# Small per-head products of a decoder step on TensorE: heads of one tile shape put side by side, sample weights on 128 partitions, squares folded twice

## What is computed

```python
s = einsum('bihd,bjhd->bijh', q, k) * exp(d)        # scores x decay: "weights"
y = einsum('bijh,bjhv->bihv', s, v) + einsum('bihd,bhdv->bihv', q, c) * exp(inter)
c_new = c * exp(b_end) + einsum('bjhd,bjhv->bhdv', k * exp(w_end), v)
...
var = square(x - mu).mean(-1)                       # LayerNorm over 1024 channels
```

## Time and profile before

| what | value |
|---|---|
| median of three runs | 1001.87 us |
| profiled execution, its own time | 997.59 us |
| its span | 995.8 us |
| granted TensorE clock, mean | 0.997 of full speed |
| TensorE matmul busy | 979.1 us (98%) |
| DVE, ACT, POOL busy | 503.0, 193.0, 81.6 us |
| layer 0: mixing block and first LayerNorm | about 32 to 206 us |
| layer 1: mixing block and first LayerNorm | about 439 to 634 us |
| experts | about 634 to 978 us |

### The profile page before, as it was taken

How to read it: one execution, slowest core, us unless ns; L and a number is a source line. 1 busy time by engine, 2 the same in 40 slices (tenths; PEclk the granted TensorE clock), 3 DMA queues, 4 the chain that set the end, 5 groups by cost and what they waited for, 6 DMA issues and landing times.

```text
span 995.8 us, 24204 instructions
## 1 busy us (share of the span) xinstructions
PE 979.1 (98%) x10904; PEld 800.4 (80%) x10904; DVE 503.0 (51%) x1032; ACT 193.0 (19%) x414; POOL 81.6 (8%) x105
## 2 busy tenths in 40 slices
PE   9999999999999999999999999999999999999995
PEld 6897887999999999997978779557776767777643
DVE  6888894755666654269878975420101201010135
ACT  1434232221111100044343332300000000000001
POOL 1110022500000000000000200230000020000020
PEclk9999999999999999999999999999999999999998
DMA  9437248224453155201243488899999999999972
GB/s 356 152 111 248 92 169 359 85 86 170 170 189 125 58 204 220 101 31 56 87 123 114 159 317 330 327 332 396 401 420 400 423 385 412 425 423 421 421 305 98
DMA packets 37500, 241.46 MB, mean 242 GB/s; under 512 B 5008, under 2 KB 8144, under 8 KB 17680
## 3 DMA queue, kind: packets, MB, share of 16 engines
q1 hardware_dynamic: 27280, 216.69, 55.4%
q0 software_dynamic: 6432, 19.43, 5.5%
q10 hardware_dynamic: 3680, 3.74, 1.2%
HBM read 228.60 MB, written 13.07 MB: 243 GB/s over the span
## 4 chain that ended last, share of the span: by engine, by line
PE 89%; DVE 8%; ACT 1%; issue 1%; DVEq 0%
PE ps L773 67%; PE ps L1384 15%; PE ps L1492 6%; PE ps L776 1%; PE ps L1321 1%; ACT up_slots L1841 0%; DVE overlay L2566 0%; DVE overlay L2512 0%; DVE small L2465 0%; ACT overlay L1841 0%; DVE overlay L2428 0%; DVE mix_or_moe L2426 0%; ACT x L1841 0%; DVE overlay L2427 0%; DVE up_slots L2546 0%
## 5 line engine op out<-in xcount | busy, mean ns | idle before, releaser
L773 PE MATMUL ps<-up_slots,mix_or_moe 128*32 128x352 f32 (+2 forms) x3248 | 241.0, 451 | 0.5 <-issue 0.4
L773 PEld LDWEIGHTS ps<-up_slots,mix_or_moe 128*32 128x32 f32 (+2 forms) x3248 | 148.5, 111 | 83.5 <-issue 10.6
L773 PE MATMUL ps<-x,up_slots 128*128 128x144 f32 (+3 forms) x832 | 152.3, 336 | 0.0
L773 PEld LDWEIGHTS ps<-x,up_slots 128*128 128x128 f32 x832 | 124.7, 190 | 25.2 <-issue 8.0
L773 PE MATMUL ps<-overlay,tables 128*32 128x256 f32 (+4 forms) x1992 | 122.6, 375 | 0.0
L773 PEld LDWEIGHTS ps<-overlay,tables 128*32 128x32 f32 (+2 forms) x1992 | 97.4, 113 | 21.2 <-issue 2.3
L3141 DVE TENSOR_TENSOR mix_or_moe<-mix_or_moe,ps 128x352 f32<-128x352 f32 x24 | 11.2, 517 | 174.7 <-PE ps L773 174.7
L1384 PE MATMUL ps<-overlay,up_slots 128*128 128x144 f32 x704 | 91.7, 286 | 0.6 <-DVE overlay L2917 0.3
L1384 PEld LDWEIGHTS ps<-overlay,up_slots 128*128 128x128 f32 x704 | 88.4, 190 | 1.1 <-issue 0.8
L773 PE MATMUL ps<-up_slots 128*128 128x144 f32 (+2 forms) x960 | 80.9, 257 | 1.2 <-DVE up_slots L2546 1.0
L773 PE MATMUL ps<-overlay,up_slots 128*128 128x128 f32 (+3 forms) x528 | 78.2, 308 | 0.0
(11 more groups left out here) (379 smaller groups left out, 1004.7 us busy)
## 6 DMA issues: line engine op xcount, KB each, us to landing
up_slots<-in_moe_w SPq DMA_DIRECT2D x64, 1408.0 KB, 22.3
overlay<-in_moe_w SPq DMA_DIRECT2D x21, 1536.0 KB, 24.1
up_slots<-in_ffn_w SPq DMA_DIRECT2D x30, 1024.0 KB, 6.9
up_slots<-in_w_in SPq DMA_DIRECT2D x27, 1024.0 KB, 5.3
up_slots<-in_w_out SPq DMA_DIRECT2D x8, 1024.0 KB, 7.0
overlay<-in_moe_w SPq DMA_DIRECT2D x7, 1024.0 KB, 23.8
mix_or_moe<-in_states POOLq DMA_DIRECT2D x6, 512.0 KB, 5.6
expert_tokens<-in_shape_tables POOLq DMA_DIRECT2D x8, 384.0 KB, 7.6
```

The costliest lines, as they stand in the source:

```text
L773: return pe.matmul(o, lhsT, rhs, start=start, stop=stop)
```

## The change

In `mix(l)` and its helpers:

- The samples' scores, decays, weights and HGRN2 intra-chunk weights of head n go to partitions 32n to 32n+31 (before: partitions 0 to 31, heads side by side in the free dimension). One product per head and one DVE or ACT operation for all four heads then stand for one per pair of heads. The tables get masks for this layout; the whole table keeps its size. The samples' values are read from `SAMPLE_VALUES` (made by `sample_rows`), and their transposes and ACT's copy of them are gone.
- Functions are split into a prompt and a sample part (`sample_scores`, `value_rows`, `key_rows`, `sample_outputs`, `sample_denominators`) and issued so that products of one tile shape follow each other.
- Panel pieces between them are joined: seven(3, 3..7) once instead of in three groups, seven(6, 0..7) in two groups instead of five, tile 16 in two instead of three. Level 5 moves ahead of the pieces of panel 3, `head_scale(C_)` of mLSTM behind HGRN2's outputs, HGRN2's sample states behind the prompt's retention states.
- `fold_squares` folds a second time (four tiles to two), and `variance` sums two tiles.

```diff
@@ variance
-                for k in range(4):
-                    last = mm(PS[:, 7, c], tb("lnmean"), SQS[q][:, k, c], k == 0, k == 3)
+                for k in range(2):
+                    last = mm(PS[:, 7, c], tb("lnmean"), SQS[q][:, k, c], k == 0, k == 1)
@@ fold_squares
-                tt(sq[:, 0:4, c], sq[:, 0:4, c], sq[:, 4:8, c], AD).then_inc(S["ln_fold"], 1)
+                link(tt(sq[:, 0:4, c], sq[:, 0:4, c], sq[:, 4:8, c], AD))
+                tt(sq[:, 0:2, c], sq[:, 0:2, c], sq[:, 2:4, c], AD).then_inc(S["ln_fold"], 1)
@@ gate_cols (TensorE)
-                    mm(PS[0:NS, C_ + 1, 0:NH], rli[:, SEQ:T], ident[:, 0:P:HR])
-                    for n in range(NH):
-                        last = mm(PS[NS * n:NS * n + NS, C_ + 1, NH:NH + 1], rtmp[:, SEQ:T], ident[:, HR * n:HR * n + 1])
+                    for k, row in enumerate((rli, rtmp)):
+                        for n in range(NH):
+                            last = mm(PS[NS * n:NS * n + NS, C_ + 1, k:k + 1], row[:, SEQ:T], ident[:, HR * n:HR * n + 1])
@@ decays
-                        mm(o[:, SEQ + P:WS], ident, tb("causal_sample"), False, False)
+                    if h0 == 0:
+                        mm(PS[:, bank, SEQ + P:WS], ident, tb("causal_sample"), False, False)
+                        mm(PS[:, bank, SEQ + P:WS], tb("headrows"), rb[:, SEQ:T], False, False)
...
-                    for o, sel, row in heads:
-                        last = mm(o[:, SEQ + P:WS], sel, row[:, SEQ:T], False, True)
@@ new
+                def sample_scores(bank, q, k):
+                    for n in range(NH):
+                        at, i = rows_of(n)
+                        r = slice(at, at + HD)
+                        last = mm(PS[NS * n:NS * n + NS, bank, SEQ + P:WS], proj[r, k + i, SEQ:T], proj[r, q + i, SEQ:T])
+                    return last
+                def sample_outputs(bank, v, w, start=True):
+                    for n in range(NH):
+                        r, p = place(n)
+                        mm(PS[r:r + HD, bank + p, SEQ:T], v(2, n), w[NS * n:NS * n + NS], start, False)
@@ order of mix(l)
-                scores(C_, QB, KB, 1, "ml_ps", "s23")
+                scores(C_, QB, KB, 1)
+                end(sample_scores(C_, QB, KB), "ml_ps", "s23")
...
-                values(B_, 0, VB, "ml_ps")
+                values(B_, VB)
                 need("ml_dv", "w23")
-                keys(C_, proj[:, KB:KB + 2], "ml_ps")
+                keys(C_, proj[:, KB:KB + 2])
+                value_rows(B_, VB, "ml_ps")
+                key_rows(C_, proj[:, KB:KB + 2], "ml_ps")
...
                 outputs(B_, value(0), 0)
-                seven(3, 3, 4)
                 outputs(B_, value(0), 1)
-                seven(3, 4, 5)
+                sample_outputs(B_, value(0), WTS)
+                denominators(C_)
                 carried(B_, state(0), QH[:, 0])
-                end(denominators(C_), "ml_ps", "out")
                 level(5, A_)
-                seven(3, 5, 7)
+                end(sample_denominators(C_), "ml_ps", "out")
+                seven(3, 3, 7)
...
-                values(B_, 2, ID, "hg_ps")
+                values(B_, ID)
...
-                scores(C_, QC, KC, 1, "ret_ps", "s23")
+                scores(C_, QC, KC, 1)
+                end(sample_scores(C_, QC, KC), "ret_ps", "s23")
+                value_rows(B_, ID, "hg_ps")
...
-                need("ml_dv", "rr")
-                head_scale(C_, RR_ML, "ml_ps")
                 need("hg_dv", "c1")
...
+                sample_outputs(B_, value(2), ATs, False)
+                need("ml_dv", "rr")
+                head_scale(C_, RR_ML, "ml_ps")
...
-                seven(6, 2, 4)
+                seven(6, 0, 4)
                 need("ret_ac", "vt")
                 need("ret_dv", "qs")
                 outputs(A_, value(1), 0)
-                seven(6, 4, 5)
                 outputs(A_, value(1), 1)
+                sample_outputs(A_, value(1), WTS)
                 end(carried(A_, state(1), QH[:, 1]), "ret_ps", "out")
-                seven(6, 5, 6)
-                need("hg_dv", "y")
-                sample_states(B_, 0, VM_HG, 2, "hg_ps")
-                seven(6, 6, 7)
+                seven(6, 4, 7)
...
+                need("hg_dv", "y")
+                sample_states(B_, 0, VM_HG, 2, "hg_ps")
@@ merge (DVE)
-                        if e >= NL - 3:
-                            n = NS // 2
-                            last = v.copy_predicated(
...
+                    if NL - 3 <= e < NL - 1:
+                        last = v.copy_predicated(right(ATs, e), right(tb("levels_sample")[:, e - NL + 3].bitcast(U32), e),
+                                                 right_only(PS[:, bank, 4 * HD:4 * HD + NS // 2], e))
```

More of the change, by code:

```diff
@@ L176, in shape_tables @@
     put("causal", np.where(j >= r[None], 0.0, NEG))
-    put("causal_sample", np.where(sample_ok, 0.0, NEG))
-    put("causal_room", np.zeros((P, SEQ)))
+    head_ok = (j % NS // DSEQ == s_i // DSEQ) & (j % NS <= s_i)
+    put("causal_sample", np.where(head_ok, 0.0, NEG))
+    same = [j % NS // (2 * s) == s_i // (2 * s) for s in LEVELS[-2:]]
+    put("levels_sample", np.stack([same[i] & (j % (2 * s) < s) & (s_i % (2 * s) >= s) for i, s in enumerate(LEVELS[-2:])]
+                                  + [j % NS == s_i], 1))
+    put("headrows", r[:, None] == HR * (r[None] // HR))
+    put("causal_room", np.zeros((P, SEQ - 3 * NS - P)))
     lg = np.log1p(-(2.0 ** (-5.0 - np.arange(NH))))
     decay = np.exp(lg[None, :, None] * np.maximum(dist, 0)[:, None, :]) * (dist >= 0)[:, None, :]
+    decay[:, 0, SEQ + P:] = np.exp(lg[r // NS][:, None] * np.maximum(s_i - j % NS, 0)) * head_ok
     put("retdecay", decay * HD ** -0.5)
@@ L1005, in denominators, with sample_denominators @@
                     for n in range(NH):
-                        mm(o[n][:, SEQ:T], onesc[0:NS, 0:HR], WT[0:NS, n, SEQ + P:WS], True, False)
+                        mm(o[n][:, SEQ:T], onesc[NS * n:NS * n + NS, 0:HR], WTS[NS * n:NS * n + NS], True, False)
+                def sample_denominators(bank):
+                    o = [PS[HR * n:HR * n + HR, bank] for n in range(NH)]
                     for n in range(NH):
@@ L1069, in level @@
                     if NL - 3 <= e < NL - 1:
[L1070 to L1074, removed]
+                        for n in range(NH):
+                            at, p = rows_of(n)
+                            r = slice(at, at + HD)
+                            last = mm(right_only(PS[NS * n:NS * n + NS, bank, 4 * HD:4 * HD + NS // 2], e), kk[r, p, SEQ:T],
+                                      right(qq[r, p, SEQ:T], e))
                     end(last, "hg_ps", f"L{e}")
                 def level_sample(bank):
[L1078 to L1081, removed]
+                    for n in range(NH):
+                        at, p = rows_of(n)
+                        r = slice(at, at + HD)
+                        last = mm(PS[NS * n:NS * n + NS, bank, 0:NS], k_hg[r, p, SEQ:T], q_hg[r, p, SEQ:T])
                     end(last, "hg_ps", "L7s")
@@ L1162, in mix @@
                 pe.wait_ge(*ev(QB + 1, l))
-                scores(B_, QB, KB, 0, "ml_ps", "s01")
+                end(scores(B_, QB, KB, 0), "ml_ps", "s01")
                 seven(1, 3, 7)
@@ L1919, in values @@
                     f(dst, PS[:, bank, :].rearrange("p (t h v) -> p t h v", t=2, h=NH), ACT.Copy)
-                    f(values_of(kind, slice(0, NS), 2), PS[0:NS, bank + 1, 0:256].rearrange("p (h v) -> p h v", h=NH), ACT.Copy)
                     end(f(SAMPLE_VALUES[kind], PS[:, bank + 1, 256:256 + HD], ACT.Copy), name, "vt")
@@ L2579, in merge_sample @@
                     need("hg_ps", "L7s")
-                    mask = tb("levels")[0:NS, NL - 1, 0:NS].bitcast(U32)
-                    for odd in range(2):
-                        last = v.copy_predicated(ATs[:, odd:NH:2], mask.unsqueeze(1).to_broadcast([NS, 2, NS]),
-                                                 PS[0:NS, 6 + odd, 0:2 * NS].rearrange("p (a i) -> p a i", a=2))
+                    last = v.copy_predicated(ATs, tb("levels_sample")[:, 2].bitcast(U32), PS[:, 6, 0:NS])
                     end(last, "hg_dv", "m7s")
```

81 lines of the change are left out of this document (37 added, 44 removed).

## The result

The changed kernel takes 990.43 us (median of four runs, 989.77 to 992.34), the kernel before 1000.85 (four runs, 996.94 to 1002.27): a ratio of 0.989, with an interval of 0.986 to 0.993. The forecast was 990.1. The profiled execution took 989.77 us, with a span of 988.0, which is 7.8 us less than the span before, and not 10.4. That gap between runs and profiles is the question of the experiments.

A forecast was written before the change was run, and what follows sets the result against it. TensorE was taken as the bound, busy 979.1 of 995.8 us. Mixing blocks 9.8 us plus LayerNorm 1.95 gave 11.8, taken from the median 1001.87: 990.1 us, range 984 to 997.

The forecast's parts named there:

- Stretch A: From level 3 to level 6's end in a mixing block: fewer instructions and tile-shape changes end it 2.2 us earlier.
- merge 6 that starts at once: On DVE after level 6: with level 5 moved earlier, merge 6 waits only for level 6, another 0.3 us.
- Stretch B: From level 6 to the retention scores: DVE sets the end, 0.2 us counts; scores start 2.7 us earlier in all.
- sign of being right: Before the retention scores: TensorE idle 0.6 us or more would show the forecast right.
- Stretch C: From the retention scores to panel 7's end: TensorE gains 2.9 us, DVE waits take some back; 2.2 taken.
- LayerNorm: Variance calls at half length through a second fold on DVE: 1.95 us over five calls.
- The sum: Whole kernel: 9.8 us from both layers' mixing blocks plus 1.95 from the variance calls, 11.8 us.
- 1 (DVE the bound in stretch C): DVE's waits line up badly there and all 2.2 us per layer are lost: 994.5 us, chance 0.12.
- 2 (one bank in series): Packed blocks of heads sharing a PSUM bank run in turn, costing 3.4 us in all: 993.5 us, chance 0.07.
- 3 (it doesn't do what it says): TensorE pauses at new output ranges, not new shapes, so joining blocks saves nothing: 999 us, chance 0.10.
- 4 (the experts' stream): Expert weights fall behind; with 7% less supply the kernel is slower, 1014 us; chance 0.05.
- experts unchanged: In the experts' stage: each expert still takes 42.6 us, a sign that the forecast is right.

The follow-up runs named there:

- t_states: HGRN2's sample states issued ahead of the prompt's retention states, against a_thin (changed kernel with expert 1's loads cut): 982.76 us, 1.1 less.
- t_single: Squares folded once and summed over four tiles again at all five LayerNorm calls, against a_thin: 985.24 us, 1.3 more.
- a_thin: Changed kernel with only 88 of 1408 columns of expert 1's first weight matrix loaded: 983.90 us, against 990.7 with all loaded.
- b_thin: Kernel before the change with only 88 of 1408 columns of expert 1's first weight matrix loaded: 994.84 us, against 1001.7 with all loaded.
- t_split: Panel pieces put back between small products (panel 3 in three groups, panel 6 in five), against a_thin: 987.26 us, 3.4 more.
- b_again: Kernel before the change, run again unchanged: 1001.69 us (12 runs, 996.44 to 1002.91).
- a_again: Changed kernel, run again unchanged: 990.71 us (989.0 to 993.34).

## Why the forecast held, and where it did not

- **Stretch A** was to end 2.2 us earlier. Level 6 ends at 86.82 instead of 89.84; less the 0.6 of the start, 2.4. The blocks came out as worked out: decays 1.39 for a forecast of 1.40, values and keys 1.32 for 1.32, outputs 1.70 for 1.68. The 0.3 for a merge 6 that starts at once came too.
- **Stretch B**: the scores start 2.9 earlier net, forecast 2.7; TensorE's wait there was forecast as 0.8, with 0.6 or more as a sign of being right; it is 0.43 in the first profile, short of that sign, and 0.43 to 1.26 in both layers of all profiles with this order.
- **Stretch C**: panel 7's end is at 144.23 instead of 149.75, 4.9 earlier net, as forecast for both stretches, so C itself gave 2.0 of 2.2; layer 1's gives 4.6 (from its level 0 on, 108.6 instead of 113.25). HGRN2's chain takes 3.04 for a forecast of 3.00, and DVE's states hold TensorE for 0.55 where 0.6 was forecast. t_states shows that this last wait was to be had for the order of two blocks.
- **LayerNorm** is the term that was mis-sized: 1.95 forecast, 1.3 measured by t_single and in the rows. The step that failed is "at (1,1) and (2,0) ... four instructions (0.54) come off and 0.3 of fold is put on: 0.26 each" (0.54 less 0.3 is 0.24). The second fold costs there what DVE needs for it, 0.49, and it came whole on top of the first: TensorE starts 0.46 later than it could and saves 0.47. At (2,0) the same stretch takes 1.84 us in a_thin and 1.87 in t_single: 0.0 each. (0,0) gave 0.36 from the products ahead of it to TensorE's restart (8.21 to 7.85) instead of 0.49, (0,1) 0.48, (1,0) 0.45.
- **The sum**, 11.8, was 10.9 to 11.0 (a_thin and b_thin), of which the cut islands are 3.3 and the folds 1.3. The other 6.3 were not taken apart by a run: products that are gone and smaller blocks side by side, block by block as above. That 990.43 came within 0.3 of 990.1 is partly luck, as the edits are worth 0.9 less than the sum and the medians of the kernel before, from one group of its runs to the next, lie between 1000.0 and 1002.3.
- **Rivals.** 1 (DVE the bound in stretch C): no, though its waits of 0.55 are real. 2 (one bank in series): no. The chunk of four heads takes 0.27 us for eight instructions (120.97 to 121.24), as forecast, and 0.87 in series. The rule of the Trainium skill, TensorEngine Tiling (Array Packing), Restrictions and Gotchas, under which they would take turns, does not agree with that; in each bank the two row groups write to different partitions here, and no run shows the case of the same ones. (The prediction's 0.27 for one such pass was read from a 128*128x128 row, a pass of the same 128 columns but of the full tile.) 3 (it doesn't do what it says): no, by t_split. 4 (the experts' stream) is half right: it does not turn the sign, but what was to show it, TensorE waiting on a DMA after 640 us, came true, and it had been dismissed by "TensorE never waits for them", read from one execution of the kernel before, one of its shorter ones, in which the list of waits names no token and no weight while the experts' part lost 3.4 us. By the medians the stream costs both kernels close to 7 us. The forecast of the median held because it costs both the same, not because it costs nothing; "experts unchanged" was the wrong reason for a right number.

What stays open: why the kernel before, unlike the changed one, also has executions (995.4 to 997.8) that the stream costs only 0.6 to 3 us. Its first profile has a hint. TensorE lost 1.6 us inside expert 0, so expert 1's first load was issued 8.0 us after expert 0's first product (641.86) and not 6.2 as in b_again (640.19), and the gather began 13.3 us after the scatter's first issue and not 17.5: the stall did what the hold does. That is one trace. What stalled TensorE there is not shown either, and no execution near 1002 was profiled.

## What to carry to other kernels

Where a stage runs with the DMA engines at a share of 1.0, a gain ahead of it can come back as a wait inside it, and one short execution, or a list of waits without a DMA in it, is no proof that it has room: cut some of the stream, and compare the two kernels without it. Small traffic in such a stage (a scatter that someone waits for, parameters that nobody needs yet) is worth an order of its own. In a TensorE-bound stretch a foreign block costs twice, in itself and in what it cuts; and a sum handed to another engine pays only where that engine is ahead.

## What had not been expected of the hardware

- An island of full-size products costs 0.30 us in all (0.14 to 0.15 in itself, 0.15 in the block that it cuts), where 0.20 had been read from the rows of the island alone.
- With TensorE idle from 650.98, the granted clock was 1.00 until 653 and 0.50 (1.2 GHz) from 654 to 660, four of these six microseconds with TensorE busy again: a wait of 5.0 us cost 7.1. Behind the wait of 3.0 in a_again expert 1's up products took 29.89 us instead of 28.57.
- The tail of an indirect scatter is slow beside streams of large loads: the last of six landed after 13.9 us, the median of the six was 8.1; with the loads held back the gather behind it began 3.7 us sooner after the scatter's first issue.
- TensorE can stand where no wait is listed: in the first profile of the kernel before it lost some 1.6 us at 640 and as much at 970, at a granted clock of 1.00, with every row in between called busy or "issue". The loss shows only against the same products in another profile.
